# Transposing normed tokens with the DMA crossbar instead of TensorE and a PSUM copy, in a bidirectional hybrid encoder block

## What is computed

```
u    = rms_norm(h, g_pre)
proj = u @ w_in                 # conv b, c, x, z | q, k, v, r, gate low-rank | merge gates a, b
p_conv = (c_b * conv3(c_c * c_x) * silu(c_z)) @ w_out_c
o      = bidirectional gated linear attention(q, k, v, gates), 4 heads, normed per head
p_gla  = (o * silu(r)) @ w_out_g
merged = sigmoid(m_a) * p_conv + sigmoid(m_b) * p_gla
out    = h + rms_norm(merged @ w_out, g_post)
```

## Time and profile before

| | us |
|---|---|
| median of 3 runs (lowest to highest) | 3068.84 (3067.51 to 3069.25) |
| the profiled execution | 3068.2 |
| its span on the slowest core (core 6) | 3066.7 |
| span over the 8 cores | 3059.2 to 3066.7 |
| granted clock, mean over the 8 cores | 0.995 to 0.997 |

### The profile page before, as it was taken

The page is one execution under the profiler, slowest core; times in us unless marked ns, Lnnn a source line. Parts: engine busy times, 40 slices in busy tenths (PEclk is TensorE's granted clock), DMA queues, the critical chain, the costliest instruction groups (busy, mean ns, idle before and its releaser), DMA issues.

```text
span 3066.7 us, 55890 instructions; the slowest of 8 cores (3059.2 to 3066.7 us)
## 1 busy us (share of the span) xinstructions
PE 2983.7 (97%) x17724; PEld 1569.0 (51%) x17724; DVE 1626.7 (53%) x2546; ACT 1425.3 (46%) x2717; POOL 835.5 (27%) x1286
## 2 busy tenths in 40 slices
PE   5999999999999999999999999999999999999998
PEld 3555554444556655444456565444445555544443
DVE  5576661542666675163276667426237766723523
ACT  5767751321567763132256776213235686512211
POOL 4233333311422222132142222223123222312122
PEclk9999999999999999999999999999999999999999
DMA  7434546732411122262341112235233111133323
GB/s 181 98 77 102 105 117 146 215 112 76 154 61 44 44 66 90 76 216 84 93 147 44 44 48 66 96 114 186 76 109 117 51 46 44 58 105 99 121 78 122
DMA packets 136733, 301.28 MB, mean 98 GB/s; under 512 B 15088, under 2 KB 18032, under 8 KB 135936
## 3 DMA queue, kind: packets, MB, share of 16 engines
q1 hardware_dynamic: 122912, 272.34, 27.5%
q0 software_dynamic: 13536, 25.37, 5.5%
HBM read 265.80 MB, written 59.31 MB: 106 GB/s over the span
## 4 chain that ended last, share of the span: by engine, by line
PE 90%; issue 2%; DVE 2%; ACT 2%; DMA 2%; POOL 1%; SPq 0%; DVEq 0%; ACTq 0%; POOLq 0%
PE ps L471 87%; PE ps L476 3%; ACT L488 1%; ACT sb_AT L488 1%; DMA sb_W<-w_all 1%; DMA sb_onT<-x 0%; DVE sb_ycX L501 0%; POOL sb_stat L645 0%; DMA sb_ycT<-x 0%; DVE sb_AT L838 0%; DVE sb_CS L501 0%; POOL sb_stat L506 0%; DVE sb_ON L506 0%; DVE sb_TB L501 0%; DVE sb_ycT L497 0%
## 5 line engine op out<-in xcount | busy, mean ns | idle before, releaser
L471 PE MATMUL ps<-sb_uT,sb_W 128*128 128x512 bf16 (+2 forms) x8960 | 1885.3, 368 | 13.1 <-ACT sb_onT L488 7.6
L471 PEld LDWEIGHTS ps<-sb_uT,sb_W 128*128 128x128 bf16 (+1 forms) x8960 | 815.2, 98 | 932.5 <-issue 35.6
L488 ACT ACTIVATE sb_CS<-ps 128x512 f32<-128x512 f32 (+1 forms) x512 | 302.7, 596 | 902.2 <-PE ps L471 901.2
L501 DVE SCALAR_TENSOR_TENSOR sb_CS<-sb_CS,ps 128x512 f32<-128x512 f32 x256 | 176.1, 688 | 686.0 <-PE ps L471 682.9
L471 PE MATMUL ps<-sb_GR 128*128 128x512 bf16 (+2 forms) x1792 | 348.8, 318 | 2.6 <-ACT sb_AT L488 2.2
L497 POOL TENSOR_TENSOR sb_GR<-sb_CS 128x512 bf16<-128x512 f32 x128 | 162.0, 1266 | 693.6 <-DVE sb_CS L501 693.5
L501 DVE SCALAR_TENSOR_TENSOR sb_CS<-sb_CS,sb_convw 128x512 f32<-128x512 bf16 x256 | 221.1, 871 | 54.3 <-ACT sb_CS L488 41.0
L471 PE MATMUL ps<-sb_V,sb_uT 128*128 128x256 bf16 x2048 | 238.3, 274 | 0.0
L471 PEld LDWEIGHTS ps<-sb_GR 128*128 128x128 bf16 x1792 | 164.0, 98 | 134.1 <-issue 3.9
L471 PE MATMUL ps<-sb_onT,sb_W 128*128 128x512 bf16 x1024 | 232.0, 379 | 0.0
L471 PEld LDWEIGHTS ps<-sb_V,sb_uT 128*128 128x128 bf16 x2048 | 198.5, 98 | 27.9 <-issue 2.0
(11 more groups left out here) (122 smaller groups left out, 2979.2 us busy)
## 6 DMA issues: line engine op xcount, KB each, us to landing
sb_W<-wsc SPq DMA_DIRECT2D x496, 256.0 KB, 2.6
sb_onT<-x SPq DMA_DIRECT2D x50, 512.0 KB, 5.6
sb_W<-w_all POOLq DMA_DIRECT2D x80, 256.0 KB, 5.7
sb_GR<-x SPq DMA_DIRECT2D x40, 512.0 KB, 5.2
wsc<-sb_W SPq DMA_DIRECT2D x80, 256.0 KB, 5.1
y<-sb_GR SPq DMA_DIRECT2D x32, 512.0 KB, 2.9
sb_ycT<-x SPq DMA_DIRECT2D x32, 512.0 KB, 4.5
y<-sb_ycT SPq DMA_DIRECT2D x32, 512.0 KB, 3.1
```

Of the source, the lines that this page charges most:

```text
L471: S.add("pe", lambda e: e.matmul(out, lhsT=lhsT, rhs=rhs, start=start, stop=stop), r, w, cost=max(0.025, free_n(rhs) / 2400.0 + 0.0025) / ...
L488: S.add("act", lambda e: e.activation(out=out, in_=in_, func=func, **kw), r, w, table=TABLE.get(func), cost=0.17 + 0.82e-3 * free_n(in_) + ...
L501: S.add("dve", lambda e: e.scalar_tensor_tensor(out=out, in0=in0, scalar=scalar, in1=in1, op0=op0, op1=op1), r, w, cost=0.21 + 1.05e-3 * f ...
```

## The change

For batches 1 to 3, `s0_tr` issues one transposing DMA on SP's queue in place of the eight TensorE transposes and the copy. It reads the bf16 tile (128 tokens by 1024 features) and writes the same 128 columns of all eight blocks of `uT`. It takes one of four semaphores by turns, and is entered in the planner with 256 KB (1 << 18 bytes). Batch 0 keeps the old way. Nothing else in the source is changed; the planner lays out the whole order anew.

```diff
+        def dtr(out, in_, r, w, semkey, nbytes):
+
+            return S.add("sp", lambda e: e.dma_start_transpose(out, in_), r, w, semkey=semkey, nbytes=nbytes)
+
...
-        def s0_tr(us, i):
+        def s0_tr(us, i, xbar):
             u_ap, u_k = us
+            if xbar:
+                dst = REG["uT"][:, :].rearrange("p (k t) -> p k t", k=8)[:, :, i * 128:(i + 1) * 128]
+                keys = [g for k in range(8) for g in uT[k](BF16, i * 128, 128)[1]]
+                dtr(dst, u_ap, u_k, keys, ("ut", i % 4), 1 << 18)
+                return
             tb, tbk = npsb()
...
-                put("ST", lambda i=i: s0_tr(us(i), i), ("ST", b, i), aft)
+                put("ST", lambda i=i: s0_tr(us(i), i, b > 0), ("ST", b, i), aft)
```

## The result

The changed kernel takes 3046.67 us (median; range 3045.0 to 3046.7) against 3069.05, a ratio of 0.9927 with a 95% interval of 0.9904 to 0.9949: 22.4 us or 0.73% less.

A forecast was written before the change was run, and what follows sets the result against it. TensorE, busy 2983.7 of 3066.7 us, was taken as the bound. From 3068.2, less 21.6 for transposes and 3 idle, plus 5 for landing waits, came 3048.6, beside the median 3049 us; range 3041 to 3058.

The forecast's parts named there:

- The removed transposes, 21.6 us: TensorE's queue: eight transposes fewer for each of 48 token tiles, 0.45 us a tile, all on the path.
- The copies, at nothing: VectorE and ScalarE: 48 of 64 copies from PSUM go, some 36 us, costed at nothing because matmuls hide them.
- Idle time credited, 3: TensorE's waits for normed tokens at the transposes: of 9.6 us idle in four windows, 3 credited as saved.
- L = 3.5 us: Assumed time from issue to landing of a 256 KB crossbar transpose on SP's queue, nearest a weight block's 2.6 us.
- rival C: Slow crossbar at the boundary: landing at 10.9 us, 75 us idle in three boundaries, 3122 us, slower than before; chance 0.17.
- A landing above 5 us: Sign named in advance that the forecast is wrong: crossbar transposes landing later than 5 us after issue.
- SP, an issue of 0.4 us and weight blocks at nothing: SP's in-order queue: loads behind transposes may come 11.4 us late before a matmul waits, so cost nothing.
- ScalarE, only the excess over the planner's price: Square of tile i+2 waits for tile i's landing; only time beyond the planner's 3.1 us stalls.
- TensorE at the boundary, 5 us: Tiles 8 to 15: landing waits at the first reader, 1.7 us per boundary, three boundaries, 5 us added.
- A: Gain lost at the boundary: ScalarE and VectorE pace 780 to 830 us, half of 21.6 stays, 3058 us; chance 0.13.
- B: Landings late by contention at boundaries: idle starts at L = 4.7; at 6.5, 22 us eats the gain, 3069; chance 0.13.
- D: Transposed write into uT breaks into tiny pieces: landing in 20 us, 61 us per boundary, over 3200 us; chance 0.03.

## Why the prediction was right, step by step

- *The removed transposes, 21.6 us.* Right: busy time fell by 22.2, to 2961.5, where the text had "near 2962".
- *The copies, at nothing.* Right in that nothing on ScalarE or VectorE became the bound.
- *Idle time credited, 3.* Too small in its place: the four windows gave 6 back. Phase 1 took 8, and the sum is 0.7 more idle time.
- *L = 3.5 us.* Too small: 4.9 in the median, 4.5, 3.9 and 4.2 at the three boundaries. At 4.2 the formula (idle from L = 4.7 on) still gives none, and TensorE waited 0.2 us for landings. The two pages of the Trainium skill come next. Eight blocks in series at the 1309 ns of VectorE: DVE Perf Modes (The three transpose paths) would be 10.5 us, an estimate, and no median of a place comes near it (the highest is 6.0, tiles 0 to 7 of batch 1), so rival C falls with it. Advanced Engine Details and Errata (X-Bar Transpose (TRN2)), "TRN2 transpose DMAs are as fast as regular DMAs", is nearer, but not met: in the same stretch of batch 1 (555 to 640 us) a weight block of the same 256 KB lands after 5.1 us in the median and a transpose after 6.0; from 770 to 850 us it is 3.7 against 4.5, from 1505 to 1600 us 3.2 against 3.9. A landing above 5 us, which I had named as a sign of being wrong, is thus common (up to 9.3); it did no harm where the reader is far off.
- *SP, an issue of 0.4 us and weight blocks at nothing.* Wrong on both: 1.2 us and more per transpose, and 3.6 us of waits for weight blocks. The cover of 11.4 us was reckoned for W2 in the conv stretch, whereas the block in question (778.56) is one for the gate projection at the boundary, through W1 with its three slots, as are the other two that TensorE waited for. Whether SP's hold or the full queue there makes it late was not told apart.
- *ScalarE, only the excess over the planner's price.* Right: 5.7 us of waits with the price, 101 without it.
- *TensorE at the boundary, 5 us.* The size was near (8 in phase 1), the place was not. I had the loop end 6 us later, covered by work drawn ahead. It was covered there; but the tokens' readers, the half-1 gate projection first, moved later, and 4.1 to 4.8 us per batch appear at the start of phase 1. That the work drawn ahead is what is missing there is my reading; the kernels with four buffers and with the transposes left out show that stretch full.
- *The sum, 3049, and the range.* 3046.7. The large term, TensorE's queue, was right in size and reason. That the idle time comes out at +0.7 where I had +2 is partly luck: -6 and +8 stand where I had -3 and +5, and the 8 in another place. The idle time of 2 to 5 us per boundary window, named as a sign of being right, was 1.9, 0.9 and 0.9.
- *Rivals.* A: the boundary pays 8.9 of 22. B: the landings were a little short of where it starts; doubled, they went well beyond. C and D did not occur.

What stays open is the part of the 11 us that four buffers do not return, and the order effects in the table above.

## What to carry to other kernels

Where TensorE is the bound, a transpose that it no longer does is worth its spacing (0.056 us per block here), not its latency of 0.22, and it is paid for in the latency of whatever loop now holds the landing. Ask which buffer the transfer still reads when the next norm wants to write it, try that loop with another buffer or two (here 4 to 11 us better alone, 11 to 14 worse beside the forward keys), and do not let the planner take the landing for free (it cost 36 us here; a price nearer the median landing was no better, it cost 8). A cost that is covered where it falls may come due later: look for idle time in the stage that used to run on the work drawn ahead.

## What was not expected of the hardware

- A crossbar transpose holds SP's queue by far longer than a plain issue and nearly whatever its size: the shortest hold is 1217 ns for 128x1024, and 1172 ns for 128x512 (the row of sb_KT above), against 0.4 us. Longer holds occur, up to 4.6 us.
- The DMA packets of the run rose from 136733 to 187419, by 50686, or 1056 for each transfer of 256 KB; those under 512 bytes from 15088 to 65776. The hardware queue's share of the 16 engines rose from 27.5 to 30.7%.
- After the same short stop of TensorE the granted clock can fall on one core and not on another. With the price up, the same program on two cores (first core 6, then core 0; windows as above):

```profile
820.00:830.00 10.00, 5.63 (x27) 2.52 (x26) 4.08 (x6) 4.58 (x9) 2.46 (x5) 0.92 0.26 68
840.00:900.00 60.00, 60.00 (x360) 33.36 (x359) 29.25 (x40) 38.34 (x62) 7.31 (x12) 0.81 0.23 59
```

```profile
820.00:830.00 10.00, 5.63 (x29) 2.56 (x28) 3.90 (x7) 4.69 (x10) 2.12 (x5) 0.95 0.23 63
840.00:900.00 60.00, 60.00 (x428) 35.49 (x426) 36.96 (x56) 43.30 (x75) 10.09 (x18) 1.00 0.26 68
```

Both idle 4.4 us between 820 and 830, as all eight cores do. Core 0 is granted the full clock (2.4 GHz) from 840 on, core 6 0.81, between the two levels, and does 360 matmuls in the 60 us in which core 0 does 428. Cores 6 and 7 alone show this; their spans are 3076.3 and 3075.2 us, those of the other six 3046.6 to 3052.7. In all five runs of 3076 to 3080 us the long spans are those of the cores with the lower mean clock, and in the four of 3055 no core has one: that is why this kernel's runs lie 25 us apart. What decides which cores it meets is not shown.
